# The low parts of the normed tiles on GpSimd instead of VectorE at two layer boundaries

## What is computed

```python
h = jnp.concatenate([meta, x], axis=1)
h = _layer_norm(h, ln_in_g, ln_in_b)
for l in range(DEPTH_2):                 # DEPTH_2 = 2
    h = _hybrid_layer(h, ...)            # input products, conv, attention, LRU, output product
                                         # ends in _layer_norm(ALPHA * h + y @ w_out, g, b)
return h[:, N_META:]
```

## Time and profile before

| | |
|---|---|
| median of three runs | 3276.13 us |
| the profiled execution, its own time | 3276.35 us |
| its span in the trace | 3274.8 us |
| mean granted TensorE clock | 0.987 of full |
| TensorE matmul busy | 97% of the span |
| VectorE busy | 67% |
| ScalarE busy | 47% |
| GpSimd busy | 10% |
| boundary 1 (n = 0) in the trace | about 1640 to 1709 us |
| boundary 2 (n = 1) | about 2453 to 2516 us |

### The profile page before, as it was taken

How to read it: one execution, slowest core, us unless ns; L and a number is a source line. 1 busy time by engine, 2 the same in 40 slices (tenths; PEclk the granted TensorE clock), 3 DMA queues, 4 the chain that set the end, 5 groups by cost and what they waited for, 6 DMA issues and landing times.

```text
span 3274.8 us, 59930 instructions
## 1 busy us (share of the span) xinstructions
PE 3178.1 (97%) x22102; PEld 2937.7 (90%) x22102; DVE 2205.9 (67%) x3031; ACT 1547.0 (47%) x2499; POOL 333.4 (10%) x341
## 2 busy tenths in 40 slices
PE   8999999999999999999979999999997999999997
PEld 7899999999999998888869999999997888887886
DVE  6677887888888886236785555556567555556647
ACT  5345555555555554232254544555236445555424
POOL 1000000000000001000001242240000214412000
PEclk9999999999999999999989999999998999999997
DMA  6244443344344345423243222223334222222422
GB/s 203 91 104 115 109 109 106 100 115 108 97 109 114 91 115 207 145 93 103 84 132 107 79 65 73 72 79 118 102 103 154 84 73 64 77 78 65 156 97 83
DMA packets 453738, 342.42 MB, mean 105 GB/s; under 512 B 20984, under 2 KB 445880, under 8 KB 450640
## 3 DMA queue, kind: packets, MB, share of 16 engines
q1 hardware_dynamic: 436032, 298.38, 30.9%
q0 software_dynamic: 8016, 24.83, 2.1%
q10 hardware_dynamic: 9552, 17.37, 1.5%
HBM read 315.04 MB, written 25.46 MB: 104 GB/s over the span
## 4 chain that ended last, share of the span: by engine, by line
PE 85%; DVE 7%; ACT 2%; DVEq 2%; issue 2%; DMA 1%; ACTq 0%; SPq 0%; POOL 0%
PE ps L681 16%; PE ps L682 16%; PE ps L683 15%; PE ps L851 8%; PE ps L854 8%; PE ps L853 8%; PE ps L1080 2%; PE ps L1121 1%; PE ps L921 1%; PE ps L687 1%; DVE w_low L1898 1%; PE ps L688 1%; PE ps L689 1%; DVE w_low_blocks L1988 1%; DVE residual L2364 1%
## 5 line engine op out<-in xcount | busy, mean ns | idle before, releaser
L681 PE MATMUL ps<-x_high,w_high 128*128 128x264 f32 (+3 forms) x3584 | 1179.8, 329 | 54.0 <-DVE w_low L1898 23.4
L682 PE MATMUL ps<-x_low,w_high 128*128 128x264 f32 (+3 forms) x3584 | 1149.8, 321 | 0.0
L683 PE MATMUL ps<-x_high,w_low 128*128 128x264 f32 (+3 forms) x3584 | 1146.7, 320 | 0.0
L681 PEld LDWEIGHTS ps<-x_high,w_high 128*128 128x128 f32 x3584 | 679.4, 190 | 113.8 <-issue 57.9
L1898 DVE TENSOR_TENSOR w_low<-w_raw,w_high 128x1024 fp32r<-128x1024 f32 x340 | 414.6, 1229 | 491.0 <-ACT w_high L1250 456.1
L682 PEld LDWEIGHTS ps<-x_low,w_high 128*128 128x128 f32 x3584 | 679.6, 190 | 53.2 <-issue 3.3
L683 PEld LDWEIGHTS ps<-x_high,w_low 128*128 128x128 f32 x3584 | 678.4, 189 | 49.2
L1250 ACT ACTIVATE w_high<-w_raw 128x1024 fp32r<-128x1024 f32 x340 | 358.7, 1057 | 323.7 <-PE ps L683 295.7
L851 PE MATMUL ps<-x_high,w_high_blocks 128*128 128x256 f32 x1600 | 456.3, 285 | 0.0
L854 PE MATMUL ps<-x_high,w_low_blocks 128*128 128x256 f32 x1600 | 449.3, 281 | 0.0
L853 PE MATMUL ps<-x_low,w_high_blocks 128*128 128x256 f32 x1600 | 449.2, 281 | 0.0
(11 more groups left out here) (443 smaller groups left out, 4191.5 us busy)
## 6 DMA issues: line engine op xcount, KB each, us to landing
w_raw_blocks<-in_w_in SPq DMA_DIRECT2D x200, 512.0 KB, 4.9
w_raw<-in_w_in SPq DMA_DIRECT2D x384, 256.0 KB, 3.1
w_raw<-in_w_out SPq DMA_DIRECT2D x280, 256.0 KB, 3.0
residual<-residual_stream ACTq DMA_DIRECT2D x8, 1056.0 KB, 11.4
residual_stream<-y_layer ACTq DMA_DIRECT2D x2, 2176.0 KB, 10.2
x_natural<-in_x SPq DMA_DIRECT2D x4, 1024.0 KB, 9.2
x_feature_major<-x_stage POOLq DMA_DIRECT2D x4, 1024.0 KB, 6.6
y_sgu_feature_major<-z_silu_g POOLq DMA_DIRECT2D x8, 512.0 KB, 5.0
```

The costliest lines, as they stand in the source:

```text
L681: pe.matmul(dst, wh[:, j, kt, wc], xh[:, k, tok], start=first, stop=False)
L682: pe.matmul(dst, wh[:, j, kt, wc], xl[:, k, tok], start=False, stop=False)
L683: return pe.matmul(dst, wl[:, j, kt, wc], xh[:, k, tok], start=False, stop=last)
```

## The change

In `norm_tiles`, VectorE no longer forms the low parts of the normed tiles. GpSimd forms them in a new function `norm_lows`, called once before layer 0 and once after the groups of layer 0: for both halves and all 16 tiles it waits for the same count of `xh_done`, does the same subtraction with the same operands, and counts up `x_ready`. That is 64 instructions in all, 32 at each boundary. The loop over tiles on VectorE ends with tile 15 and not two tiles later. Each call stands on GpSimd's queue behind `parameters` and ahead of the wait of line 610.

```diff
+            def norm_lows(n):
+
+                for q, c in enumerate(COLS):
+                    for d in range(KT):
+                        pool.wait_ge(xh_done, (3 + 3 * n + q) * KT + d + 1)
+                        pool.tensor_tensor(xl[:, d, c], y2[:, d, c], f(xh[:, d, c]), ALU.subtract).then_inc(x_ready, 1)
+
             pool.wait_ge(acc_in, 48)
             parameters(0)
+            norm_lows(0)
...
                     parameters(l + 1)
+                    norm_lows(l + 1)
...
-            def norm_tiles(n, q, split, beside):
+            def norm_tiles(n, q, beside):

                 c = span(n)[q]
-                for d in range(KT + 2 if split else KT):
-                    if d < KT:
-                        if d % 4 == 0:
-                            dve.drain()
-                        dve.tensor_tensor(res[:, d, c], res[:, d, c], lrb[:, c], ALU.mult).then_inc(ln_t, 1)
-                        if d + AHEAD < KT:
-                            center(n, q, d + AHEAD)
-                    if split and d >= 2:
-                        e = d - 2
-                        dve.wait_ge(xh_done, (3 + 3 * n + q) * KT + e + 1)
-                        dve.tensor_tensor(xl[:, e, c], y2[:, e, c], f(xh[:, e, c]), ALU.subtract).then_inc(x_ready, 1)
+                for d in range(KT):
+                    if d % 4 == 0:
+                        dve.drain()
+                    dve.tensor_tensor(res[:, d, c], res[:, d, c], lrb[:, c], ALU.mult).then_inc(ln_t, 1)
+                    if d + AHEAD < KT:
+                        center(n, q, d + AHEAD)
                     beside(d)
```

More of the change, by code:

```diff
@@ L2424, in beside @@
                         norm_local(n, 1)
-                norm_tiles(n, 0, K is not None, beside)
+                norm_tiles(n, 0, beside)
                 norm_spread(n, 1)
@@ L2437, in finish @@
                     low(K + 1, 3)
-                norm_tiles(n, 1, K is not None, lambda d: None)
+                norm_tiles(n, 1, lambda d: None)
             dve.drain()
```

## The result

| | before | after |
|---|---|---|
| median | 3277.14 us (3275.14 to 3279.79, nine runs) | 3286.63 us (3284.65 to 3288.93, nine runs) |
| ratio | 1 | 1.0029, 95% interval 1.002 to 1.0037 |
| the profiled execution | 3276.35 us, span 3274.8 | 3288.93 us, span 3287.4 |

The change costs 9.5 us. I had forecast +3.2 us and "no change". By the prediction's own line of 0.2% (6.5 us) the kernel is slower, to which it gave a chance of 0.22. The time lies inside the stated range (3272 to 3287) and outside the narrower one of the forecast case (3275.5 to 3285).

A forecast was written before the change was run, and what follows sets the result against it. VectorE's instruction stream was taken to bound half 0 at each boundary, TensorE waiting behind it. Terms 0.65 + 0.95 + 2 x 0.4 + 0.8 = +3.2 us gave 3279.3 us, no change; range 3272 to 3287.

The forecast's parts named there:

- the forecast case: Whole kernel: GpSimd's reads and VectorE's two-operand instructions exclude each other; +3.2 us, 3279.3 us, own range 3275.5 to 3285, chance 0.52.
- The bound, the chain and the place to watch: Half 0: VectorE's stream bounds; tile 13's multiply, ScalarE's three tiles, last low part, then TensorE, whose last-piece start matters.
- the last piece: TensorE's final piece of half 0, forecast to start 37 to 38.5 us after the first multiply (37.05 before, boundary 1).
- the chain's end: End of half 0: GpSimd's 0.70 us low part replaces VectorE's 0.45 us, +0.25 us at each boundary.
- Side by side: Rival at the boundaries: exclusion doesn't bite on 272-column instructions; -7.2 us, 3268.9 us, faster; chance 0.12.
- VectorE keeping its turn: Rival in half 0: GpSimd gets in at drains only; about +1.5 us, 3277.6 us, no change; chance 0.21.
- The hold: Boundaries: time one GpSimd low part stops VectorE, taken as 0.45 us, bounds 0.40 and 0.55.
- dearer GpSimd: Rival, both halves: low part takes 0.90 us, holds VectorE 0.65; +7.6 on top of 3.2, 3287 us, slower; chance 0.15.
- The drains: Half 0: low parts falling on VectorE's drains save 0.16 us each; 10 of 13 at boundary 1, 8 at boundary 2.
- Half 1: Values' unit: last low part 0.5 to 1.5 us later, 0.6 covered by TensorE's slack; 0.4 us lost at each boundary.
- The clock: TensorE after the pause ahead of half 0's last piece: +0.8 us, bounds 0.9 us won to 3.6 us lost.
- the same ledger: Half 0 sum of holds, removed low parts, drains and chain end: +0.65 us at boundary 1, +0.95 at boundary 2.

The follow-up runs named there:

- GpSimd only counting: Changed kernel with GpSimd's subtraction replaced by a bare count of x_ready, so no engine forms the normed tiles' low parts; 3268.91 us, ratio 0.9976.
- the kernel with PSUM operands: Changed kernel with mean and scale of the first two norms left in PSUM, where ScalarE writes them in place; 3277.68 us, ratio 1.0001.
- the last kernel: Changed kernel with mean and scale in PSUM, extra matmuls in TensorE's pause, and half 1's local statistics moved behind tile 15's multiply; 3272.53 us, ratio 0.9985.

## Why the prediction was right and wrong

**The bound, the chain and the place to watch** were right: VectorE's stream, then ScalarE over three tiles, then one low part; new waits of TensorE for GpSimd ahead of the last piece and in half 1. What was removed was priced right (3.87 us; measured 3.89 and 3.52), and GpSimd's instruction nearly so (0.70 with bounds 0.67 to 0.76; 0.77 on 272 columns where nothing holds it up). Its 0.07 us over the estimate is most of the miss at the chain's end, +0.34 against +0.25. Each term that depends on how the two engines share was too small.

**The exclusion holds on short instructions too.** VectorE's and GpSimd's timelines in half 1 at boundary 1:

```profile
1705.62 0.41 DVE L2373 TENSOR_TENSOR residual<-residual,norm_mean_bc 128x256 f32<-128x256 f32 x1
1705.95 0.95 DVE L2387 TENSOR_TENSOR residual<-residual,norm_scale_bc 128x256 f32<-128x256 f32 x1
1706.83 0.41 DVE L2373 TENSOR_TENSOR residual<-residual,norm_mean_bc 128x256 f32<-128x256 f32 x1
1707.16 0.96 DVE L2387 TENSOR_TENSOR residual<-residual,norm_scale_bc 128x256 f32<-128x256 f32 x1
...
1705.69 0.93 POOL L608 TENSOR_TENSOR x_low<-y_layer,x_high 128x256 fp32r<-128x256 f32 x1 [0.61 <-ACT x_high L1596]
1706.90 0.94 POOL L608 TENSOR_TENSOR x_low<-y_layer,x_high 128x256 fp32r<-128x256 f32 x1 [0.28 <-ACT x_high L1596]
```

GpSimd asks at 1705.69 while the centring reads, waits for it (0.93 us instead of 0.73), and then holds up the multiply, which takes 0.95 us instead of 0.41. This settles two rivals. Side by side is out. VectorE keeping its turn is out too: its multiply was issued right behind the centring, and GpSimd got in between them. The Trainium skill, "SBUF — State Buffer", section "Who interferes with whom", states which instructions conflict: a VectorE instruction with two SBUF inputs conflicts with a GpSimd instruction that reads SBUF and not with one that only writes, and with at most one SBUF input, outside the modes that use both ports, it does not conflict. The runs agree on all three counts (longest multiply 1.007, 0.443 and 0.439 us).

**The hold was 0.54 to 0.57 us, not 0.45.** In the lines above it is 0.95 - 0.41 = 0.54 on 256 columns; on 272 it is 1.00 - 0.43 = 0.57. I had taken 0.45 from the long pairs of the earlier trace rows, with 0.55 as a bound. The 0.14 us between 0.43, my value for a GpSimd instruction that has itself waited, and 0.57 have two halves. GpSimd's instruction takes 0.77 us and not 0.70. And VectorE's own work begins 0.13 us before GpSimd's end and not 0.20: in the lines above GpSimd ends at 1706.62 and the multiply at 1706.90, which less 0.41 is 1706.49. So the "dearer GpSimd" rival, which set the point of decision at a hold of 0.54 and an instruction of 0.79 us, was right for one half of the difference; a low part of 0.90 us, as it had it, isn't there.

**The drains covered fewer turns.** I put 10 of 13 on a drain at boundary 1 and 8 of 13 at boundary 2. Where a turn did fall on a drain, the cover of 0.16 us was right: the instruction takes 0.82 (L2352 in the chain above) and not about 1.0. But of the 13 lengthened VectorE instructions at boundary 1 only five lie at 0.82 to 0.84 us; six take 0.93 to 1.01, and two are tensor_scalars. At boundary 2 it is four of eleven. The excesses of the 13 over their lengths alone add up to 6.0 us, and the stretch is 5.89 us longer than with GpSimd only counting. I had expected 5.85 - 1.6 = 4.25 us. That gives half 0 its +2.34 and +2.48 us against the +0.65 and +0.95 of the forecast: 3.2 of the 6.3 us that were missing.

**Half 1 cost 1.4 us at each boundary, not 0.4.** I had put the shared path at 1.1 us per tile against ScalarE's 0.99; GpSimd's starts above are 1.21 us apart. The last low part ends 18.90 us after the first multiply of half 1 instead of 16.81, so 2.1 us later and beyond my 0.5 to 1.5; TensorE had 0.6 of that in hand. It is the same hold again, and another 2 us.

**The clock** was forecast at +0.8 us in all with 3.6 as the bound; two executions showed +3.65 and +0.5. The pause and its effect on the last piece were foreseen, the size wasn't knowable from the rows, and four traces of that pause don't settle it.

Sum by the measured terms: 2.34 + 2.48 + 2.8 = 7.6 us, with the clock 8.1 to 11.3; measured 9.5. The mechanism was right, and the hold, the turns on drains and half 1 were mis-sized. With a hold of 0.55 us and 5 and 4 turns on drains the same ledger would have given +2.7 and +2.9 for half 0 and, its other terms kept, +7.2 in all: slower. The range held the result only because it was widened to take in half of the "dearer GpSimd" case; that it did so is in part luck, and the last piece at 39.39 us lies outside the 37 to 38.5 that were to show the forecast case.

## What to carry to other kernels

Moving an elementwise operation from VectorE to GpSimd frees VectorE only if what stays on VectorE beside it doesn't read two operands from SBUF; here most GpSimd instructions of 0.73 to 0.77 us cost VectorE 0.40 to 0.57, more than the 0.35 of doing it itself. Look at the operands of what stays on VectorE: with one of them in PSUM the same move cost nothing. When sizing such a hold from two rows of long instructions, carry its upper bound through the whole ledger: 12 or 13 turns at each boundary made 0.1 us decisive.

## What was not expected of the hardware

- A tensor_scalar with one SBUF tensor is held up as well. It takes 0.35 us alone, and beside GpSimd's reads (VectorE's timeline of the changed kernel):

```profile
1651.36 0.67 DVE L2467 TENSOR_SCALAR residual<-acc,par 128x256 f32<-128x256 f32 x1
```

  In the kernel with PSUM operands it reached 0.78 us. The Trainium skill's section named above lists tensor_scalar among the operations that can use both ports and so conflict; I had counted only instructions with two operands.
- The turns alternate: a waiting GpSimd instruction gets in between two VectorE instructions issued back to back.
- The same pause ahead of the last piece, of the same length, was followed by a pass of 11.24 and 10.20 us in one execution and of 9.81 and 8.49 in the next. Filling it with matmuls brought 8.50 at both boundaries, with no delay to the piece behind. In the last kernel, where the pause was shorter, the same matmuls delayed that piece by 0.4 us.
